# A two-block transformer and recurrence kernel: chunk copies, low parts and one wait around the down projection change place

## What is computed

```python
h2 = rmsnorm(x, g_ffn[l]) * (1.0 + sc2) + sh2
gate, up = jnp.split(h2 @ w_gu[l], 2, axis=-1)
x = x + ga2 * ((jax.nn.silu(gate) * up) @ w_down[l])      # w_down: 2816 x 1024
return rmsnorm(x, g_final)
```

## Time and profile before

| | before |
|---|---|
| median of 3 runs | 1038.04 us (1034.44 to 1039.26) |
| profiled execution, its own time | 1037.87 us |
| its span, first to last instruction | 1036.0 us |
| TensorE busy | 1011.6 us (98%) |
| VectorE busy | 757.8 us (73%) |
| ScalarE busy | 509.1 us (49%) |
| GpSimd busy | 502.6 us (49%) |
| mean granted TensorE clock | 0.996 of full speed |

### The profile page before, as it was taken

How to read it: one execution, slowest core, us unless ns; L and a number is a source line. 1 busy time by engine, 2 the same in 40 slices (tenths; PEclk the granted TensorE clock), 3 DMA queues, 4 the chain that set the end, 5 groups by cost and what they waited for, 6 DMA issues and landing times.

```text
span 1036.0 us, 15847 instructions
## 1 busy us (share of the span) xinstructions
PE 1011.6 (98%) x5814; PEld 844.5 (82%) x5814; DVE 757.8 (73%) x1423; ACT 509.1 (49%) x781; POOL 502.6 (49%) x207
## 2 busy tenths in 40 slices
PE   6999999999999999999999999999999999999997
PEld 5687787677887999999978877888887778888886
DVE  6368997786775555655599597799999999885322
ACT  4243325885356565565742213525436878353232
POOL 0034342692427757557354335247855666633440
PEclk9999999999999999999999999999999999999999
DMA  9994222150222432332389832234231323223212
GB/s 325 349 292 142 82 87 77 42 164 1 82 82 82 126 118 81 120 124 81 108 289 300 287 113 81 82 119 124 88 116 40 99 75 112 83 82 121 81 41 81
DMA packets 127385, 128.98 MB, mean 124 GB/s; under 512 B 3680, under 2 KB 125408, under 8 KB 127328
## 3 DMA queue, kind: packets, MB, share of 16 engines
q1 hardware_dynamic: 126080, 127.38, 38.3%
q10 hardware_dynamic: 1248, 0.86, 0.3%
HBM read 126.13 MB, written 2.10 MB: 124 GB/s over the span
## 4 chain that ended last, share of the span: by engine, by line
PE 62%; issue 18%; POOL 11%; DVE 3%; ACT 2%; DMA 2%; SPq 1%; POOLq 0%; DVEq 0%; ACTq 0%
PE bank L821 13%; PE bank L823 13%; PE bank L822 13%; POOL w_lo L661 4%; POOL w_a L753 3%; POOL w_hi L753 2%; PE bank L1168 2%; PE bank L1139 2%; PE bank L1011 2%; POOL w_s L762 2%; PE bank L1456 1%; PE bank L1458 1%; PE bank L1457 1%; DMA ada_stage<-in_w_ada 1%; PE bank L1414 1%
## 5 line engine op out<-in xcount | busy, mean ns | idle before, releaser
L661 POOL TENSOR_TENSOR w_lo<-w_stage,w_hi 128x2048 fp32r<-128x2048 f32 x59 | 282.0, 4780 | 378.1 <-ACT w_hi L1529 373.4
L821 PE MATMUL bank<-act_hi,w_hi 128*128 128x512 f32 x544 | 216.2, 397 | 1.2 <-ACT tmp L1781 1.1
L823 PE MATMUL bank<-act_hi,w_lo 128*128 128x512 f32 x544 | 211.8, 389 | 0.0
L822 PE MATMUL bank<-act_lo,w_hi 128*128 128x512 f32 x544 | 211.8, 389 | 0.0
L1529 ACT ACTIVATE w_hi<-w_stage 128x2048 fp32r<-128x2048 f32 x60 | 114.7, 1912 | 148.7 <-PE bank L823 136.4
L2726 DVE SCALAR_TENSOR_TENSOR bank<-v_pad,vcol,bank 128x512 f32<-128x512 f32 x208 | 138.2, 746 | 0.0
L821 PEld LDWEIGHTS bank<-act_hi,w_hi 128*128 128x128 f32 x544 | 102.1, 188 | 28.2 <-issue 4.9
L822 PEld LDWEIGHTS bank<-act_lo,w_hi 128*128 128x128 f32 x544 | 102.2, 188 | 21.9 <-issue 1.4
L823 PEld LDWEIGHTS bank<-act_hi,w_lo 128*128 128x128 f32 x544 | 102.1, 188 | 21.7
L821 PE MATMUL bank<-ff_hi,w_hi 128*128 128x512 f32 x176 | 71.4, 406 | 2.9 <-DVE ff_lo L2560 2.2
L823 PE MATMUL bank<-ff_hi,w_lo 128*128 128x512 f32 x176 | 69.7, 396 | 0.0
(11 more groups left out here) (401 smaller groups left out, 2524.7 us busy)
## 6 DMA issues: line engine op xcount, KB each, us to landing
w_stage<-in_w_in SPq DMA_DIRECT2D x29, 1024.0 KB, 5.2
ada_stage<-in_w_ada SPq DMA_DIRECT2D x20, 1024.0 KB, 11.5
w_stage<-in_w_gu SPq DMA_DIRECT2D x14, 1024.0 KB, 5.1
w_stage<-in_w_out SPq DMA_DIRECT2D x12, 1024.0 KB, 5.2
late_stage<-in_mod_w SPq DMA_DIRECT2D x12, 1024.0 KB, 9.3
w_stage<-in_w_gu SPq DMA_DIRECT2D x16, 512.0 KB, 3.5
w_stage<-in_w_down SPq DMA_DIRECT2D x8, 1024.0 KB, 5.6
late_stage<-in_w_ada SPq DMA_DIRECT2D x4, 1024.0 KB, 11.0
```

The lines of the kernel that those rows point to most:

```text
L661: nc.gpsimd.tensor_tensor(w_lo[b][:], w_stage[b][:], w_hi[b][:].bitcast(F32), ALU.subtract).then_inc(s_lo, 1)
L821: pe.matmul(dst, wh, rhs_hi(k), start=(first and k == 0), stop=False)
L822: pe.matmul(dst, wh, rhs_lo(k), start=False, stop=False)
L823: mm = pe.matmul(dst, wl, rhs_hi(k), start=False, stop=(last and k == n_k - 1))
```

## The change

Five edits. `DOWN_HIGH` loses its entry for k = 3: the copy of down chunk 8 (`after(C_DOWN + 6)`) moves to k = 4, and the copy of down chunk 11 (`after(C_DOWN + 9)`) leaves k = 6 and goes to the front of `undivided_high(5)`. In the last round ScalarE's copy of down chunk 1 moves behind `high_silu(1)`. VectorE's low part of tiles 8 to 12 moves ahead of the last `right_product`, and the last two low parts move ahead of a dozen small steps on `lam_t`. TensorE's second pair of gate tiles waits for VectorE's `s_div` where it waited for ScalarE's `s_silu`.

```diff
-DOWN_HIGH = {0: (0, 1, 2, 3), 2: (4, 5), 3: (6,), 4: (7,), 5: (8,), 6: (9, 10)}
+DOWN_HIGH = {0: (0, 1, 2, 3), 2: (4, 5), 4: (6, 7), 5: (8,), 6: (10,)}
...
-                        pe.wait_ge((s_silu, s_up)[q], j * 2 + (1 + m))
+                        if (j, q) == (1, 0):
+                            pe.wait_ge(s_div, 2 + m)
+                        else:
+                            pe.wait_ge((s_silu, s_up)[q], j * 2 + (1 + m))
...
                     ff_high(8, 12)
                     ff_high(12, 16)
-                    hi_part(C_DOWN + 1, (C_DOWN + 1) % 2, stage_uses(C_DOWN + 1))
                 high_silu(1, made + (CV0 + (8 if last else 9)))
...
+                    hi_part(C_DOWN + 1, (C_DOWN + 1) % 2, stage_uses(C_DOWN + 1))
                     ff_high(16, 20)
...
                 if k == RAW_FROM:
+                    after(C_DOWN + 9)
                     act.wait_ge(s_mod, 10)
...
                     out_low_right(1, at + (PROD0 + 12))
+                    ff_low(8, 12, 3)
                     right_product(t + 1, 1, silu + (SG0 + 3))
...
-            ff_low(8, 12, 3)
-            ff_low(12, 16, 4)
+            for q, (t0, t1) in enumerate(((12, 16), (16, 20), (20, KF))):
+                ff_low(t0, t1, q + 4)
...
-            ff_low(16, 20, 5)
-            ff_low(20, KF, 6)
```

## The result

The changed kernel takes 1030.50 us (median of 5 runs, 1030.17 to 1030.76), the kernel before 1037.72 in the same comparison: ratio 0.9933, interval 0.9917 to 0.9949. The profiled execution took 1030.76 us with a span of 1029.0; forecast were 1031.2.

The account below looks back on a forecast made before the run. TensorE, busy in 98% of the span, was taken as the bound. Gains of 0.76 + 1.15 + 3.16 + 0.72 + 0.61 = 6.40 us, plus some 0.3 for restarts, gave 1037.87 - 6.7 = 1031.2 us; range 1028.8 to 1035.5.

Parts of the forecast that it names:

- Gate: Second gate tile: without the silu wait, TensorE restarts 0.06 us after GpSimd, at 316.33 in place of 317.09; gain 0.76 us.
- Low parts and chunks 1 and 2: Down projection: reordered low parts turn stops of 1.48 and 0.74 us into one of about 1.1; gain 1.15 us.
- The second rival: Ahead of down chunk 1: VectorE's queued low parts hold GpSimd throughout; 1032.6 us, or 1034.2 with a clock fall; chance 0.11.
- Late chunk 10: Down projection: squares of tile 3 no longer wait behind a copy, so the 1.58 us stop goes; 3.16 us with clock.
- the clock's 1.58: Behind the stop at late chunk 10: without that stop the granted clock no longer falls; gain 1.58 us.
- Chunk 11 and the sums: Late down projection: chunk 11's copy about 3.7 us earlier removes stops of 0.72 us and, at the sums of squares, 0.61.
- Sum: Whole run: five gains total 6.40 us; with some 0.3 us for four fewer restarts, 6.7 us.
- the restart: After each TensorE stop: first matmul drawn 0.08 to 0.11 us longer, some 0.3 us for four restarts fewer.
- The first: Second block: VectorE sets the pace and takes the gain back, so the end stays at 1037.9 us; chance 0.10.
- third: Late chunk 10 still late, because an earlier late chunk or the squares wait for something else; 1034.4 us; chance 0.11.
- fourth: The new stop ahead of chunk 2 drops the clock to 1.2 GHz for long, priced at 30 us; 1046 us; chance 0.04.

Follow-up runs that it names:

- the fold moved: Kernel before, with VectorE's small operations folding the last modulation into `scale` placed behind the update of `xT` of token tile 5; 1035.69 us.
- the squares undone: Changed kernel with ScalarE's copy of down chunk 8 again ahead of the squares of token tile 3; 1032.82 us.
- chunk 11 alone: Kernel before, with only ScalarE's copy of down chunk 11 moved ahead of the copies of the last token tile's activations; 1035.25 us.
- the squares alone: Kernel before, with only ScalarE's copy of down chunk 8 moved behind the squares of token tile 3; 1032.18 us.
- lower group: Unchanged kernel: 22 of its 59 runs over all comparisons, at 1034.0 to 1035.2 us; the other 37 took 1037.1 to 1039.3 us.
- chunk 2 earlier: Changed kernel with ScalarE's copy of down chunk 2 also moved ahead of its logarithm; 1028.89 us, ratio to before 0.9925.
- the gate undone: Changed kernel with the gate's wait on ScalarE's silu put back; 1031.04 us.
- before, again: Kernel before, unchanged, run twice more with traces; 1034.78 and 1037.54 us.
- the stop filled: Kernel before, with small unread products on TensorE in the idle stop ahead of the late products of chunk 10; 1037.83 us.

## Why the prediction was right, and where not

The time was right within 0.7 us, and most of the steps with it.

**Gate: right.** 0.76 us forecast, 0.76 read, 0.76 in the three lowest runs of its undo (0.98 in the median).

**Low parts and chunks 1 and 2: right.** GpSimd got in behind the running instruction and ended chunk 1 at 523.87 (524.5 forecast), the low parts ended at 527.16 (527.8), two stops became one of 1.15 us (1.07). The gain is 1.26 us, not 1.15. The second rival did not occur: GpSimd started at 519.37 between two of VectorE's low parts. But VectorE was not ready with the next one, it waited 0.41 us for ScalarE's `ff_hi`; that GpSimd also gets in where the next is ready rests on the second pair of the earlier trace rows.

**Late chunk 10: the stop right, the clock half right.** The stop went, with 7.5 us to spare. The step that failed is "with the stop gone, the clock's 1.58": I took the fall as the stop's fixed companion, from one trace. Six traces have this stop of 1.58 us: the fall is in two of the three of the kernel before and in that with the fold moved, but not in the third of the kernel before, nor in those with the squares undone or chunk 11 alone. None of the eight traces in which this stop is gone or filled has a fall there. So in these traces the fall there goes with the stop, but doesn't always come with it.

**Chunk 11 and the sums: right in total, wrong in cause.** I read the stop as the copy's place behind six copies. It was VectorE's fold, held by GpSimd in both traces of the kernel before in which the clock had fallen; 3.30 us stood in the trace of before, at 624.56, on an engine that I had not followed back from the copy. So 0.72 and 0.61 us were no terms of their own edit: the squares alone give 116.08 - 110.88 = 5.20 us, and undoing the chunk-11 edit costs nothing. That their sum came out is luck: I priced them apart and didn't know that these losses lie on one chain, of which the changed kernel has none. The squares move the chain forward, away from the collision: GpSimd's low half of chunk 10 begins at 614.48 where it began at 623.22, and is over at 619.10, ahead of the fold.

```profile
614.48 4.62 POOL L661 TENSOR_TENSOR w_lo<-w_stage,w_hi 128x2048 fp32r<-128x2048 f32 x1 [4.54 <-ACT w_hi L1532]
...
619.39 0.17 DVE L2221 SCALAR_TENSOR_TENSOR scale<-mod,vcol 128x8 f32<-128x8 f32 x1
```

**Sum.** 6.7 us forecast, 7.0 read in the span. The term that was undersized is the restart, for which I gave 0.1 us. Matmuls are drawn 0.39 us long and start 0.23 apart, so a bracket, which counts from the drawn end, leaves out 0.16 us of every stop. At late chunk 10 the lower group's trace takes 2.77 us from the last product ahead of the stop to the second one behind the late sums (598.71 to 601.48), the changed kernel 0.91 (596.89 to 597.80): the stop costs 1.86 us, its 1.58 and 0.17 of overlap and 0.11 of longer first matmuls. At chunk 2 it is 1.42 us for a bracket of 1.15, of the 1.48 that go with chunk 2 earlier (gate to sums 330.32 in place of 331.80). Four restarts fewer so give some 0.6 us more than I counted, where the forecast lacks 0.4 us by the profiled executions and 0.7 by the median.

**Rivals.** The first is excluded by the last column of the table, 380.7 against 380.6 us: nothing is taken back in the second block. The third and fourth did not occur. A rival was missing: that the trace of before showed the worse of two outcomes. Against the lower group the same change gives 1034.4 - 1030.5, about 4 us, within the 0.5% that I called no difference; the ratio rests on which group the median of before falls in.

**Open.** What decides, in one program, whether the clock falls at the stop, and why single runs of other kernels (the gate undone, chunk 2 earlier) have a lower mean clock; those runs have no traces, but the one with the fold moved shows that falls come at other places too. The Trainium skill (TensorE: Matmul & The Clock Gate, "Part 1: The HAM clock gate") has the chip judge TensorE's activity over a window that runs free of the program, so that one program can fare differently from run to run; the traces agree so far that one program shows both outcomes after the same stop, and no run here shows that window.

## What to carry to other kernels

When a kernel's times come in groups, take the trace of each before pricing an edit: a term read from one of them may be an accident that one edit removes and another only covers. From a stop, follow the chain back through every engine until an instruction is much longer than its kind; here a 0.17 us operation at 3.30 us, three engines away, was the cause. And if several edits lie on one such chain, their prices don't add: undo each alone and do each alone.

## What the runs showed of the hardware

A small operation of VectorE on 128x8 elements (0.16 to 0.17 us alone) stood for 2.66 to 4.63 us when it met GpSimd's 128x2048 subtraction, and GpSimd's was drawn 5.86 us in place of 4.62 when it met VectorE's 128x2048 low part. Each time the small operation ended with GpSimd's instruction (in the second trace of before, again, 624.30 + 3.33 = 627.63 against 627.61). The Trainium skill (SBUF — State Buffer, "Who interferes with whom") has it that a VectorE instruction with two SBUF inputs and a GpSimd instruction that reads SBUF contend for one port, which the first keeps for its whole instruction; the traces agree. The page lists tensor-scalar operations among those that can take both ports, and L2685, one of them with a single tensor, was held for 4.63 us like those with two. What I had not expected is how little decides: drawn 0.02 us behind GpSimd, this operation was held in the trace with the stop filled and not held (0.16 us) in the lower group's.

The granted clock fell to 0.50 behind stops of 1.58 us in three of six traces, and behind one of 2.02 us in the window of 642 to 644 us. With the stop of 1.58 us filled by products that nobody reads it stood at 1.00 in the one trace; that the filling did it isn't shown, since three traces with the stop stand at 1.00 as well.
